# Two transformer blocks with split fp32 weights on one Trainium2 core: 36 low weight parts of the mixing stages computed by GpSimd instead of the vector engine

## The reference, cut to what matters

```python
x = x + 0.5 * swiglu(rmsnorm(x, g1), wg1, wu1, wd1)      # d_ff 2816
h = rmsnorm(x, gm); proj = h @ w_in
# block one: neighbourhood attention (8 heads) and gated linear attention (4 heads)
# block two: forgetting + dilated attention (4 + 4 heads) and a gated recurrence (HGRN2, 4 heads)
x = x + concat([attention, recurrence]) @ w_out
x = x + 0.5 * swiglu(rmsnorm(x, g2), wg2, wu2, wd2)
```

## Time and profile before

| what | value |
|---|---|
| time, median of 3 runs | 2288.98 us (2287.17 to 2290.28) |
| span of the profiled execution, first to last instruction | 2281.4 us |
| the profiled execution's own time | not given apart from the three above, whose median is 7.6 us above the span |
| PE busy | 2191.0 us (96%) |
| DVE busy | 1769.9 us (78%) |
| ACT busy | 990.3 us (43%) |
| POOL busy | 49.1 us (2%) |
| DVE, low parts (L866) | 332 of 2291 ns mean, 753.6 us |
| mean granted clock of PE | 0.984 |

### The profile page before, as it was taken

The page is one execution under the profiler, slowest core; times in us unless marked ns, Lnnn a source line. Parts: engine busy times, 40 slices in busy tenths (PEclk is TensorE's granted clock), DMA queues, the critical chain, the costliest instruction groups (busy, mean ns, idle before and its releaser), DMA issues.

```text
span 2281.4 us, 44799 instructions
## 1 busy us (share of the span) xinstructions
PE 2191.0 (96%) x17544; PEld 2100.2 (92%) x17544; DVE 1769.9 (78%) x1769; ACT 990.3 (43%) x1050; POOL 49.1 (2%) x56
## 2 busy tenths in 40 slices
PE   7999989999999999999899999999999999989998
PEld 6999879999999898999899988899989998879998
DVE  7877787877888696878788877678778787777786
ACT  4333564333433455433433353543344335354332
POOL 4000003000000000000000000000000000000000
PEclk9999999999999999999999999999999999899999
DMA  9454326454454433454354432244444543324541
GB/s 302 174 189 166 112 93 179 166 195 155 185 184 165 148 112 121 180 189 165 129 200 168 181 127 100 93 167 165 183 158 185 190 169 130 111 75 150 199 168 37
DMA packets 51214, 357.32 MB, mean 157 GB/s; under 512 B 6480, under 2 KB 6912, under 8 KB 8352
## 3 DMA queue, kind: packets, MB, share of 16 engines
q1 hardware_dynamic: 47952, 349.20, 41.7%
q0 software_dynamic: 2288, 5.25, 1.1%
q10 hardware_dynamic: 864, 1.39, 0.2%
HBM read 354.77 MB, written 1.05 MB: 156 GB/s over the span
## 4 chain that ended last, share of the span: by engine, by line
PE 83%; DVE 9%; issue 3%; ACT 2%; DVEq 2%; ACTq 0%; DMA 0%
PE bank L349 51%; PE bank L359 26%; DVE w_lo L866 2%; PE bank L435 1%; PE bank L375 1%; DVEq L1064 1%; DVE x L890 1%; PE bank L476 1%; DVE arena L1026 1%; DVE arena L976 1%; DVE arena L929 1%; PE bank L515 1%; DVE h_lo L899 1%; PE bank L479 0%; DVE stat L1188 0%
## 5 line engine op out<-in xcount | busy, mean ns | idle before, releaser
L349 PE MATMUL bank<-h_hi,w_hi 128*128 128x256 f32 x3392 | 972.5, 287 | 27.5 <-DVE h_lo L899 19.5
L349 PE MATMUL bank<-h_lo,w_hi 128*128 128x256 f32 x3392 | 965.4, 285 | 0.0
L349 PE MATMUL bank<-h_hi,w_lo 128*128 128x256 f32 x3392 | 965.1, 285 | 0.0
L866 DVE TENSOR_TENSOR w_lo<-raw,w_hi 128x2048 fp32r<-128x2048 f32 x332 | 753.6, 2291 | 161.9 <-ACT w_hi L594 160.4
L594 ACT ACTIVATE w_hi<-raw 128x2048 fp32r (+1 forms) x332 | 632.2, 1906 | 239.7 <-PE bank L349 187.7
L349 PEld LDWEIGHTS bank<-h_hi,w_hi 128*128 128x128 f32 x3392 | 656.6, 194 | 39.9 <-DVE h_lo L899 21.6
L349 PEld LDWEIGHTS bank<-h_lo,w_hi 128*128 128x128 f32 x3392 | 657.1, 194 | 0.2
L349 PEld LDWEIGHTS bank<-h_hi,w_lo 128*128 128x128 f32 x3392 | 656.7, 194 | 0.0
L359 PE MATMUL bank<-act_hi,w_hi 128*128 128x256 f32 x1280 | 363.9, 284 | 0.0
L359 PE MATMUL bank<-act_lo,w_hi 128*128 128x256 f32 x1280 | 362.3, 283 | 0.0
L359 PE MATMUL bank<-act_hi,w_lo 128*128 128x256 f32 x1280 | 362.3, 283 | 0.0
(11 more groups left out here) (194 smaller groups left out, 2046.2 us busy)
## 6 DMA issues: line engine op xcount, KB each, us to landing
raw<-stream SPq DMA_DIRECT2D x332, 1024.0 KB, 4.8
arena<-rpb POOLq DMA_DIRECT2D x32, 96.0 KB, 9.3
x<-xt ACTq DMA_DIRECT2D x1, 1024.0 KB, 6.7
out<-x SPq DMA_DIRECT2D x1, 1024.0 KB, 3.9
arena<-c_level POOLq DMA_DIRECT2D x1, 896.0 KB, 10.0
arena<-c_att POOLq DMA_DIRECT2D x1, 512.0 KB, 8.3
arena<-code_w POOLq DMA_DIRECT2D x2, 128.0 KB, 5.0
scratch<-positions ACTq DMA_DIRECT2D x1, 128.0 KB, 2.7
```

The source lines that it names most:

```text
L349: last = mm(o, a, r, start=(k == 0 and j == 0), stop=(k == KC - 1 and j == 2))
L866: tt(w_lo[s][:, :], raw[s][:, bass.ds(n % RAW, 1), :].rearrange("p a n -> p (a n)"), w_hi[s][:, :].bitcast(F32), ALU.subtract).then_inc(lo ...
```

## The change

The low parts of the late steps leave the DVE's queue. POOL's queue gets a loop over them, behind the bias mask in each layer of block one and behind the small loads in each layer of block two. The arithmetic and the buffers are the same.

```diff
+LATE = [range(3, len(MIX1) - 1), range(3, len(MIX2) - 1)]
...
+            def mixing_low(b, L):
+                for i in LATE[b]:
+                    s, n = mix_use(b, L, SPLIT_ORDER[b][i + 3])
+                    pool.wait_ge(hi_done[s], n + 1)
+                    pool.tensor_tensor(w_lo[s][:, :], raw[s][:, bass.ds(n % RAW, 1), :].rearrange("p a n -> p (a n)"),
+                                       w_hi[s][:, :].bitcast(F32), ALU.subtract).then_inc(lo_done[s], 1)
...
                     .then_inc(bias_masked, 1)
+                mixing_low(0, L)
...
                     .then_inc(small_loaded, 16)
+                mixing_low(1, L)
...
-                    late = i < nunits - 1 and (i in SPAN_AFTER[b] or i in ITEM_AFTER[b] or (b == 1 and i >= 3))
-                    if not late and i < nunits - 1:
+                    if i not in LATE[b] and i < nunits - 1:
                         split(*mix_use(b, L, SPLIT_ORDER[b][i + 3]))
...
-                    if late:
-                        split(*mix_use(b, L, SPLIT_ORDER[b][i + 3]))
```

## The result

The changed kernel takes 2371.71 us (median, 2367.98 to 2376.72), the kernel before 2288.07 us: **ratio 1.0364, 95% interval 1.0346 to 1.0382**, slower by 84 us. The forecast was 2373 us, within 2335 to 2405. The profiled execution is the slowest of the four, with a span of 2374.8 us.

The account below looks back on a forecast made before the run. TensorE was taken as the bound (83% of the last-ending chain), DVE nearly as full in block one. Block one +53 and block two +31 make 84 us: span 2365, plus 7.6, 2373 us; range 2335 to 2405.

Parts of the forecast that it names:

- GpSimd's price: Each low part of 2048 elements on GpSimd: 4.52 us, scaled from two 3072-element operations, against 2.28 us on DVE.
- The hold: GpSimd operations on SBUF and DVE instructions with two SBUF inputs do not run side by side; the first one finishes.
- The upper bound with L1186 and L1188 held: High case in block one: these DVE instructions are held too, 1.45 us in each of 16 steps, +23 us, 2396 us.
- Block one, 12.3 us a step: Late steps of block one: a closed GpSimd, DVE, ACT chain makes 8.97 us 12.3, +3.3 in 16 steps, +53 us.
- Block two, 31 us: Ten late steps a layer of block two, in three kinds, together 15.7 us a layer, +31 us for two.
- Gates: First two late steps of a block two layer: GpSimd gets in between DVE's scans, +9.0 us, with no slack.
- those that TensorE covers: Next five late steps of a block two layer: 6.5 us of room for a 4.52 us hold, so no cost.
- The last three: Last three late steps of a block two layer: no DVE wait, 2.2 us each, 6.7 us.
- the rival without a hold: GpSimd works beside DVE; TensorE bounds, 4 us won in block one, some 2 in block two: 2283 us; chance 0.05.
- some 2 us in block two: Gain in block two, where the low part stood ahead of a span, if GpSimd does not hold DVE.
- TensorE's clock: New idle time of 3 us a step may lower it; fits block one's 3.6 us TensorE wait, so nothing added.
- The 7.6 us around the span: Amount by which the runs' median lies above the profiled span, added to 2365 to give 2373 us.

Follow-up runs that it names:

- the gated kernel: Changed kernel with block two's first two low parts a layer on DVE, the other 32 waiting for DVE's two-input work to end: 2284.83 us, ratio 0.9984 to the kernel before.
- the memset: Changed kernel with GpSimd's subtraction replaced by a one-column subtraction and a write-only fill of the other 2047 columns: 2284.02 us, ratio 0.9981 to the kernel before.
- alone it measured 46.6: Changed kernel with only block one's 16 low parts on GpSimd, block two's 20 back on DVE: 2334.98 us, ratio 1.0208 to the kernel before.
- alone 33.4: Changed kernel with only block two's 20 low parts on GpSimd, block one's back on DVE: 2321.8 us, ratio 1.0161 to the kernel before.

## Why the prediction was right, and where not

- **The total** is nearer (84 us forecast, 84 measured) than its two terms: block one came out 5 us cheaper than forecast by the marks (6 by the medians), block two 5 us dearer by the marks (2 by the medians). That they cancel is luck.
- **GpSimd's price**, 4.52 us from two rows of another shape: 4.60 undisturbed, 4.65 in the mean. The waits had been taken off rightly; the fixed part of 0.2 us was missed.
- **The hold.** L940's 7.40 us and L931's 3.83 in the trace before were the whole case, in two rows. The changed kernel's scans (11.09 us), L1037 (5.66) and L1179 (3.59) show it again, and the gated kernel shows that it is the hold and not GpSimd's slowness or a late low part that costs. The prediction spoke of any GpSimd operation on SBUF; the memset shows that for two-input instructions it has to be one that reads. By the page "SBUF — State Buffer" of the Trainium skill, section "Who interferes with whom", a DVE instruction in a 2-port mode is held too, and one with at most one SBUF input outside these modes is not. The trace agrees on the second: L1178, with one input from PSUM, took its 0.69 us beside GpSimd. L1201, a TENSOR_SCALAR, took 4.61 us instead of 0.17, which fits the first, but no run here shows that a port mode is the reason. The upper bound with L1186 and L1188 held is out: in the gated kernel their like took 0.75 and 0.69 us beside GpSimd.
- **Block one, 12.3 us a step**: measured 12.3, by the chain as it was written down. The term made of it, 16 x 3.3 = 53 us, was too large: the mixing parts grew by 23.9 + 24.2 = 48.1 us, and alone it measured 46.6. The chain needs a step before and behind it. Eight operations close only seven periods (L1073's from 269.69 to L1071's copy at 355.92: 86.2 us, where the seven of before took 62.9), 3.3 us each or 23.3 a layer. The first operation cost only 1.5 us, in the step ahead.
- **Block two, 31 us**: alone 33.4, by the marks 36. In the first layer, from the start of the scans (1358.61, now 1415.11), the terms were all off. Gates: 9.0 forecast, with no slack; the scans took 8.65 us more, but the first span's copy came only 6.7 us later (1368.61, now 1431.84), since two of DVE's own low parts in front of it were gone. The third low part was put among those that TensorE covers; it held L1041 (4.86 instead of 0.69 us) ahead of the second span, and its step grew by 2.6 us. The steps of the four behind it changed by +2.8, -1.5, 0.0 and +1.7 us, so the middle five cost 5.5 us where nothing was forecast. The last three cost 4.4, 6.7 forecast.
- **What DVE's relief is worth**: 6 us in the rival without a hold, 10.5 measured when the low parts were left out. What was mis-sized there is "some 2 us in block two", which was 6.5 by the marks.
- **TensorE's clock** was to fall without cost in block one. Its granted clock in the late steps went from 1.00 to 0.89, so partly to 1.2 GHz, while the period stayed what the other three engines' chain gives: 11.9 us from 285.59 at a granted clock of 1.00, 12.35 us from 297.53 at 0.79, and in both no row of the chain waited for TensorE. In block two, where TensorE bounds the middle steps, it has a price that the forecast did not have. While GpSimd held the scans TensorE ran no matmul for 4.84 us and had a granted clock of 0.55 in the 6.29 us behind, mostly 1.2 GHz. In the step that begins with the second span's copy its 81 matmuls were busy for 14.76 us at 0.78, before for 12.83 at 0.87; the step after that won 1.5 us back, at 1.00 instead of 0.87:

```profile
1420.71:1425.55 4.84, 0.00 (x0) 0.00 (x0) 4.84 (x3) 0.00 (x0) 4.37 (x1) 0.88 0.60 217
1425.55:1431.84 6.29, 3.62 (x19) 3.62 (x20) 3.52 (x7) 2.25 (x3) 0.00 (x0) 0.55 0.49 169
1441.02:1456.61 15.59, 14.76 (x81) 12.91 (x82) 6.93 (x14) 6.99 (x11) 4.53 (x1) 0.78 0.24 93
```
```profile
1375.23:1388.06 12.83, 12.83 (x81) 11.38 (x80) 8.40 (x15) 5.75 (x9) 0.00 (x0) 0.87 0.30 93
```

The first three lines are of the changed kernel, the last of the kernel before. How much of the 16.3 and 20.0 us is the clock's in all is not separated.
- **The 7.6 us around the span** were not what lies around it: in the changed kernel that is 1.9 us (2376.72 against 2374.8). The profiled execution of before was a quick one, and its bias mask fell on the cheap place; whether that is the whole difference to the median is not shown. The sum came out right because a difference was added to a median.

## What to carry to other kernels

Before moving an elementwise operation from DVE to GpSimd, look for one row in the trace where the two overlap: if DVE's two-input instructions end with GpSimd's, the move can add up to GpSimd's length to every chain that such an instruction (here also a TENSOR_SCALAR) is on, whatever the load of either engine, and only a wait for something else hides it. Then the start of the operation is what counts: a wait that puts it beside DVE's PSUM reads and reductions turned +3.3% into -0.2% here. And ask what DVE's time is worth first; a version that leaves the work out altogether gave 10 us where 82 us of DVE work were removed.

## What was not expected of the hardware

- An instruction on two numbers a row is held as long as a large one: L1201 took 4.61 us beside GpSimd (0.17 alone), and ACT's softmax waits for it. Where GpSimd starts 0.1 us later, L1201 slips through and L1037 is held instead. The steps differ in length (L1073 starts at 282.41, 294.04, 307.08 and 318.51 us, 11.6, 13.0 and 11.4 us apart), but not by which of the two was held: it was L1037 in the first and L1201 in both others.
- GpSimd, too, waits for a DVE instruction that is running, and takes its turn between two of them: it got in after the first scan, let one scan through, and got in again (the scans end at 1415.81, 1420.79, 1425.63 and 1426.21 us, GpSimd's two operations at 1420.25 and 1425.08). Neither engine starved the other here.
- The same GpSimd operation costs more or less by where it happens to fall: the bias mask is in both kernels, and the part around it took 199.4 us before and 204.3 in the changed kernel, where the mask started 0.4 us earlier.
